# A hybrid diffusion step on one core: the last expert scatter handed over bank by bank, and the final norm computed on turned rows

## The reference, cut to what matters

```python
def rmsnorm(x, g):
    xf = x.astype(jnp.float32)
    y = xf * lax.rsqrt(jnp.mean(xf * xf, axis=-1, keepdims=True) + EPS)
    return (y * g.astype(jnp.float32)).astype(x.dtype)
...
    for i in range(DEPTH):
        ...
        hc2 = rmsnorm(xc, norm2_g[i]) * (1 + ac2) + sc2
        hl2 = rmsnorm(xl, norm2_g[i]) * (1 + al2) + sl2
        xc = xc + gc2 * moe(hc2, router_w, router_b, moe_wg[i], moe_wu[i], moe_wd[i])
        xl = xl + gl2 * moe(hl2, router_w, router_b, moe_wg[i], moe_wu[i], moe_wd[i])
    y_prompt = rmsnorm(xc, final_g)
    y_sample = rmsnorm(xl, final_g)
```

## Time and profile before

| | us |
|---|---|
| median of 3 runs | 1867.9 |
| lowest and highest | 1867.45, 1869.59 |
| profiled execution | 1866.5 |
| its span in the trace | 1864.7 |
| TensorE busy | 1771.1 (95%) |
| VectorE busy | 476.1 (26%) |
| ScalarE busy | 385.3 (21%) |
| moved by DMA | 609.47 MB, 327 GB/s in the mean |

### The profile page before, as it was taken

How to read it: one execution, slowest core, us unless ns; L and a number is a source line. 1 busy time by engine, 2 the same in 40 slices (tenths; PEclk the granted TensorE clock), 3 DMA queues, 4 the chain that set the end, 5 groups by cost and what they waited for, 6 DMA issues and landing times.

```text
span 1864.7 us, 21714 instructions
## 1 busy us (share of the span) xinstructions
PE 1771.1 (95%) x8838; PEld 1034.5 (55%) x8838; DVE 476.1 (26%) x1240; ACT 385.3 (21%) x774; POOL 40.6 (2%) x52
## 2 busy tenths in 40 slices
PE   4999999999999988999999999999999999999996
PEld 2677544446745867854444747864444687544444
DVE  1242511115300242241111244350111252411112
ACT  1232200003102472110001232320000342200002
POOL 1000000000000000000000000000000000000000
PEclk9999999999998988999999999989999999899998
DMA  9979699997998225379999895869999819699992
GB/s 323 365 284 387 261 422 427 427 418 275 354 368 300 99 105 202 140 286 428 427 426 415 313 332 208 328 243 424 427 427 422 311 67 383 250 423 426 427 426 96
DMA packets 134407, 609.47 MB, mean 327 GB/s; under 512 B 12486, under 2 KB 19278, under 8 KB 109473
## 3 DMA queue, kind: packets, MB, share of 16 engines
q1 hardware_dynamic: 117264, 589.32, 79.4%
q10 hardware_dynamic: 12528, 10.70, 1.8%
q0 software_dynamic: 4512, 8.02, 1.1%
HBM read 606.15 MB, written 8.92 MB: 330 GB/s over the span
## 4 chain that ended last, share of the span: by engine, by line
PE 87%; DVE 4%; DMA 3%; ACT 3%; issue 1%; ACTq 1%; DVEq 0%; SPq 0%; POOLq 0%
PE PS L1535 23%; PE PS L961 22%; PE PS L1546 12%; PE PS L1499 7%; PE PS L991 4%; PE PS L1043 3%; PE PS L1011 2%; DVE arena L2085 2%; DMA ring<-in_moe_wg 1%; PE PS L1540 1%; PE PS L1479 1%; DMA ring<-in_w_mod 1%; PE PS L1029 1%; DVE RS L1696 1%; PE PS L1521 1%
## 5 line engine op out<-in xcount | busy, mean ns | idle before, releaser
L1535 PE MATMUL PS<-ring,arena 128*64 128x512 f32 x1280 | 375.5, 601 | 1.6 <-DMA ring<-in_moe_wg 1.5
L893 ACT ACTIVATE arena<-PS 128x512 f32<-128x512 f32 (+1 forms) x130 | 70.6, 543 | 797.7 <-PE PS L1526 349.9
L1535 PEld LDWEIGHTS PS<-ring,arena 128*64 128x64 f32 x1280 | 116.9, 138 | 179.2 <-issue 179.1
L2085 DVE TENSOR_TENSOR arena<-arena,PS 128x512 f32<-128x512 f32 x32 | 33.5, 1046 | 638.9 <-PE PS L1535 638.9
L961 PE MATMUL PS<-HS,ring 128*128 128x256 f32 x768 | 176.6, 388 | 3.0 <-DVE HS L1788 1.7
L1535 PE MATMUL PS<-arena 128*64 128x512 f32 x576 | 169.6, 594 | 0.0
L961 PEld LDWEIGHTS PS<-HS,ring 128*128 128x128 f32 x768 | 147.0, 194 | 30.2 <-issue 8.6
L1499 PE MATMUL PS<-arena 128*128 128x256 f32 (+3 forms) x688 | 144.6, 361 | 5.1 <-ACT arena L893 3.7
L961 PE MATMUL PS<-arena,ring 128*128 128x256 f32 x640 | 140.1, 381 | 2.5 <-ACT arena L659 1.1
L1546 PE MATMUL PS<-ring,arena 128*64 128x512 f32 x640 | 141.7, 595 | 0.0
L1499 PEld LDWEIGHTS PS<-arena 128*128 128x128 f32 (+1 forms) x688 | 112.2, 190 | 44.2 <-issue 22.7
(11 more groups left out here) (341 smaller groups left out, 1711.9 us busy)
## 6 DMA issues: line engine op xcount, KB each, us to landing
ring<-in_w_mod SPq DMA_DIRECT2D x48, 2048.0 KB, 15.7
ring<-in_moe_wu SPq DMA_DIRECT2D x41, 2048.0 KB, 21.0
ring<-in_moe_wd SPq DMA_DIRECT2D x41, 2048.0 KB, 21.6
ring<-in_moe_wg SPq DMA_DIRECT2D x41, 2048.0 KB, 20.3
arena<-in_moe_wg SPq DMA_DIRECT2D x24, 2048.0 KB, 18.1
HS<-in_moe_wu SPq DMA_DIRECT2D x12, 2048.0 KB, 18.3
arena<-in_moe_wu SPq DMA_DIRECT2D x12, 2048.0 KB, 20.3
arena<-in_moe_wd SPq DMA_DIRECT2D x12, 2048.0 KB, 24.9
```

The costliest lines, as they stand in the source:

```text
L893: A(dst, src, func).then_inc(S(sem), 1)
L1535: ins = mm(PS[64 * e:64 * e + 64, b, :], XG[:, k, 64 * e:64 * e + 64], w[:, k], start=(k == 0), stop=(k == KD - 1))
L2085: tt(by_k(HID), row(SG), row(bank(here[1])), ALU.mult).then_inc(S("hid"), 1)
```

## The change

- The eight matmuls of a scatter gave one increment, at the end, in each of the 32 pairs. Now only the last scatter of a layer increments the semaphore, once for each bank, after every second matmul, and the residual waits for the count that covers its column tile. The wait for extra blocks' scatter stays ahead of the residual.
- The final norm no longer uses norm and sumsq. TensorE turns X itself, column tile by column tile as the residual delivers it, into rows in banks 4 to 7 (two banks for each stream). ScalarE squares each bank of 512 with an accumulator, which gives a sum for each token on its own partition. VectorE adds the two sums of a token, ScalarE takes the root of two values a partition, VectorE the reciprocal, and then multiplies each bank in PSUM by that scalar and by final_g, writing to XR. Each stream is stored after its two banks.
- final_g is not loaded as a column at the start, but at the end, to all 128 partitions (512 KB), into slot 0 of the weight ring, by SyncE, once TensorE is through with the last weights, and in SyncE's stream behind the wait for the extra blocks.

```diff
@@ SyncE
-            sp.wait_ge(S("y_sb"), 4)
-            sp.dma_start(O["y_prompt"][0], XR[:, 0]).then_inc(S("out"), 16)
-            sp.dma_start(O["y_sample"][0], XR[:, 1]).then_inc(S("out"), 16)
+            sp.wait_ge(S("down"), 2 * NPAIR * DEPTH)
+            sp.dma_start(FG, I["final_g"].partition_broadcast(P)).then_inc(S("load_b"), 16)
+            for s, y in enumerate(("y_prompt", "y_sample")):
+                sp.wait_ge(S("y_sb"), 2 * s + 2)
+                sp.dma_start(O[y][0], XR[:, s]).then_inc(S("out"), 16)
@@ ScalarE
-            for name, src, n in (("cc", I["c_ctx"], 8), ("cl", I["c"][0], 8), ("fin", I["final_g"], 8),
+            for name, src, n in (("cc", I["c_ctx"], 8), ("cl", I["c"][0], 8), 
...
-            norm(2 * DEPTH)
-            act.wait_ge(S("back"), 32 * DEPTH)
-            for k in range(KD):
-                act.wait_ge(S("xn"), KD * 2 * DEPTH + k + 1)
-                run(A(H[:, k], H[:, k], ACT.Copy, scale=prm("fin", 1, k)), "h0")
-            for j in range(4):
-                c, s = j // 2, j % 2
-                act.wait_ge(S("yT"), j + 1)
-                run(A(XR[:, s, 512 * c:512 * c + 512], bank(2 * s + c), ACT.Copy), "y_sb")
+            run(A(sm(636, 1)[0:1], eps1, ACT.Sqrt), "scalar")
+            for j, (s, c) in enumerate(((0, 0), (1, 0), (0, 1), (1, 1))):
+                act.wait_ge(S("yT"), 2 * c + s + 1)
+                run(A(SQ[:, 0:2].rearrange("p a b -> p (a b)"), bank(4 + 2 * s + c), ACT.Square, accum_out=YSS[:, s, c:c + 1]), f"y_sq{j}")
+            after(act, "y_sum")
+            run(A(YR, YSS[:, :, 0], ACT.Sqrt, bias=c_("eps"), scale=1.0 / D), "y_root")
@@ TensorE
-                    if t == 7:
-                        ins.then_inc(S(sem), 1)
+                        if sem and t % 2:
+                            ins.then_inc(S(sem), 1)
...
-            sumsq(2 * DEPTH)
-            for c in range(2):
-                pe.wait_ge(S("h0"), KD * 2 * DEPTH + 4 * c + 4)
+            for k in range(KD):
+                pe.wait_ge(S("x"), KD * 2 * DEPTH + k + 1)
                 for s in range(2):
-                    for k in range(4 * c, 4 * c + 4):
-                        ins = tp(bank(2 * s + c, P * (k % 4), P * (k % 4) + P), H[:, k, T * s:T * s + T], ident)
-                    ins.then_inc(S("yT"), 1)
+                    ins = tp(bank(4 + 2 * s + k // 4, P * (k % 4), P * (k % 4) + P), X[:, k, T * s:T * s + T], ident)
+                    if k % 4 == 3:
+                        ins.then_inc(S("yT"), 1)
@@ VectorE
-            def residual(sem, base, l, vec, src):
+            def residual(sem, base, l, vec, src, each=1):
 
                 for m in range(KD):
-                    if sem:
-                        v.wait_ge(S(sem), base + m + 1)
+                    v.wait_ge(S(sem), base + m // each + 1)
...
-                v.wait_ge(S("scatter"), n0 + 8)
                 v.wait_ge(S("x_scatter"), before + nx)
-                residual(None, 0, l, 5, lambda m: bank(m // 2, N2 * (m % 2), N2 * (m % 2) + N2))
+                residual("scatter", 4 * l, l, 5, lambda m: bank(m // 2, N2 * (m % 2), N2 * (m % 2) + N2), each=2)
...
-            norm(2 * DEPTH)
+            after(v, "y_sq3")
+            run(tt(YSS[:, :, 0], YSS[:, :, 0], YSS[:, :, 1], ALU.add), "y_sum")
+            after(v, "y_root")
+            run(v.reciprocal(YR, YR), "dve")
+            v.wait_ge(S("load_b"), 64)
+            v.wait_ge(S("back"), 32 * DEPTH)
+            for s in range(2):
+                for c in range(2):
+                    run(stt(XR[:, s, 512 * c:512 * c + 512], bank(4 + 2 * s + c), YR[:, s:s + 1], FG[:, 512 * c:512 * c + 512], ALU.mult, ALU.mult), "y_sb")
```

More of the change, by code:

```diff
@@ L179 @@
     "vector_step": ["zero_rows", "prm", "a_ropek0", "l_abs", "l_rows", "l_ac", "g_sm", "g_am0", "g_am1", "g_am2", "g_at_sb0", "g_at_sb1", "g_rn0", "g_rn1",
-                    "a_ropek3"],
-    "scalar_step": ["cs", "l_rowexp", "l_n_sb", "l_nT_sb", "g_u_sb", "g_se", "g_gate", "g_root0", "g_root1"],
+                    "a_ropek3", "y_sum"],
+    "scalar_step": ["cs", "l_rowexp", "l_n_sb", "l_nT_sb", "g_u_sb", "g_se", "g_gate", "g_root0", "g_root1", "y_sq0", "y_sq1", "y_sq2", "y_sq3", "y_root"],
 }
@@ L300, in program @@
         ROOM = [ring[:, r].rearrange("p a b -> p (a b)") for r in range(RING)] + [arena[:, 9608 + 4096 * e:13704 + 4096 * e] for e in range(2)] + [HS[:, :].rearrange("p a b c -> p (a b c)")]
+        FG = ROOM[0][:, 0:D]
+        YSS, YR = sm(0, 2, 2), sm(8, 2)
         MP = [ar(8000, 512), ar(8000, 512), ar(12288, 512), sq(1536, 512), ar(8000, 512)]
@@ L463, in load @@
                 if n == 1:
-                    sp.wait_ge(S("load_p"), 16 * 12)
+                    sp.wait_ge(S("load_p"), 16 * 11)
                     sp.wait_ge(S("load_x"), 32)
@@ L972, in _ @@
             pe.nop().then_inc(S("x_scatter"), 1)
-            pe.wait_ge(S("load_p"), 16 * 12)
+            pe.wait_ge(S("load_p"), 16 * 11)
             for j in range(3):
@@ L1547, in down, with scatter @@
                     return ins
-                def scatter(par, sem, first=False, ts=range(8)):
+                def scatter(par, sem=None, first=False, ts=range(8)):
                     for t in ts:
@@ L1573, in pair @@
                             pe.wait_ge(S("ys"), 2 * n)
-                            scatter(1 - par, "scatter", first=(i == 1), ts=range(6))
+                            scatter(1 - par, first=(i == 1), ts=range(6))
                     if more and not first:
@@ L1579, in pair @@
                     if not first:
-                        scatter(1 - par, "scatter", first=(i == 1), ts=range(6, 8))
+                        scatter(1 - par, first=(i == 1), ts=range(6, 8))
                     if more:
@@ L1634, in moe @@
                         ins.then_inc(S("x_down"), 1)
-                        pe.wait_ge(S("scatter"), q0 + 8)
+                        pe.wait_ge(S("scatter"), 4 * (l + 1))
                         pe.wait_ge(S("x_a"), x_step(before, i, "x_ys"))
```

## The result

The changed kernel took 1849.24 us in the median of 4 runs (1847.65 to 1853.81), the kernel before beside it 1868.74 (1867.45 to 1870.73): ratio 0.9899, 95% interval 0.9880 to 0.9918. Two later comparisons of the same two kernels gave 0.9931 (0.9903 to 0.9958) and 0.9928 (0.9909 to 0.9947); over all of them the medians are 1854.5 (14 runs) and 1868.0 (83 runs), 13.6 us apart. The ratios are each from one comparison; the pool mixes comparisons that ran on different chips. So two things want explaining: what the change is worth, and where the rest of the first 19.5 came from.

What follows compares the result with a forecast made beforehand. TensorE carries 87% of the chain, so gains lie where it runs dry: passages 5.0, end 6.3 and start 0.2 sum to 11.5 us, taking the median from 1867.9 to 1856.4. Range 1853.0 to 1861.5, 8 in 10.

Steps and rivals of the forecast that it cites:

- Passages: Three passages from a layer's experts to the next layer's norm: bank signals save 5.0 us, bounds 0 and 8.4.
- ScalarE is late next: In the passages, ScalarE's Sqrt table limits the first square, leaving gains of 1.60, 1.53 and 1.79 us.
- the rival of 2.8 us a passage: Passages: were ScalarE free earlier, the scatter limits and up to 2.8 us each is won, 1853; chance 0.05.
- The end: From last residual to last store: new final norm and stores save 6.3 us, bounds 4.2 and 7.3.
- The stores' term: End of program: y_prompt's store gets 1.6 us of lead, so the second's wait shortens by 0.7 us, bounds 0 and 1.3.
- The rival of a final norm that is not shorter: End: squares and scalings out of PSUM cost 1.5 us each, adding 4.5 us, 1860.9; chance 0.05.
- final_g: Late 512 KB broadcast load before the final scalings: costs nothing, with 9.5 us of cover; beyond that, one for one.
- The rival on the other side: End: final_g's broadcast lands late, up to 29.6 us, giving 1876.5; chance 0.04 for eating the gain, 0.06 for later still.
- The start: Program start: without final_g's column load ahead of it, x_sample may land sooner; 0.2 us less, bounds 0 to 0.4.
- Weight waits: Experts' weight stream: waits for loads swallow the passages' gain, leaving 6.5 us, 1861.4; chance 0.12 with idle bank signals.
- the prediction's sign of being wrong: In a later layer: TensorE waiting more than 1.5 us for a weight would show the forecast wrong.
- The sum and its range: Whole kernel: 11.5 us less than the median 1867.9, so 1856.4; range 1853.0 to 1861.5 to hold 8 in 10.

Runs made afterwards that it cites:

- e6: Changed kernel with ScalarE's part of the extra blocks left out in layers 0 to 2; ratio to the kernel before 0.9912 (5 runs).
- e2: Kernel before with only the new final norm and its late load of final_g, scatter handed over whole; 1860.14 us, ratio 0.9965.
- e7: Changed kernel with one part undone: both stores wait for all four scalings; single execution, 1848.98 us.
- e9: Changed kernel, unaltered, measured and traced a third time against the kernel before; ratio 0.9928.
- e10: Kernel before, unaltered, measured against itself and traced a third time; ratio 0.9984.
- e5: Changed kernel with 23 dummy products on TensorE where it stands idle; 1849.85 us against 1865.65 for the kernel before, ratio 0.9913.

## Why the prediction was right or wrong

- **Passages: mis-sized, 5.0 for 6.5.** The mechanism held and the first squares came when it said. The step that failed was "as both go at 0.52 a column": 0.52 was VectorE's pace, which ScalarE had followed in the earlier trace rows. Freed from it, squares are 0.45 apart, 0.5 us less over eight, in each of three passages: 4.9 + 3 x 0.47 + the 0.2 of layer 0's slip make about 6.5. The trace of before had that pace, in its first norm:

```profile
41.74 3.55 ACT L606 ACTIVATE HS<-X 128x256 f32<-128x256 f32 x8
```

  And that "ScalarE is late next" was only half of it: TensorE's sums behind its scatter are late within 0.1 us of the same time, as e6 shows. By that the rival of 2.8 us a passage, with ScalarE free, falls too.
- **The end: right.** 6.3 forecast, 6.55 in the trace, 6.5 in e2. Squares 0.72 (0.72), scalings 0.78 (0.79), the last store's issue 5.9 us after the residual's last column (6.0). The stores' term was 0.9 (0.7), by e7. The rival of a final norm that is not shorter, with dear operations out of PSUM, did not occur.
- **final_g: right.** Hidden; landed in 3.7 us, whole. The rival on the other side had no ground. Of the Trainium skill's two statements ("DMA: Bandwidth & Descriptors") neither was tested for its own sake. In the load's two busiest us, 1831.4 to 1833.4, the 16 DMA engines were busy for 0.77 and 0.75 in the mean, so more than a few took part; that all sixteen did is not shown.
- **The start: 0.2 forecast, nothing found.** x_sample was issued sooner (7.33 for 7.60) and landed 10.3 us later instead of 9.7; TensorE took it up at 17.62, after 17.37 before. So its landing did not follow its issue, here or in the other traces (10.1 to 10.3 without final_g's load ahead, 9.4 to 9.8 with it). The 1.15 us by which the changed kernel led at the first norm came again only in e7 (47.25), and not in its own other traces (48.72 and 48.86, against 48.38, 49.38 and 48.71).
- **Weight waits: a rival that hardly mattered.** For the up weights TensorE waited 3.1 us in all where it had been 1.5, in three places: 1.3 ahead of the first passage, 1.6 in layer 1, 0.2 in layer 2. The 1.6 is 0.1 past the prediction's sign of being wrong, but the kernel before waited 2.7 and 3.3 us in its other traces, and between the passages the stretches grew by 0.4 us or less where a passage gave 2.1. That the 1.5 was the only wait for a weight was not so: the trace of before has 6.3 us more for ring<-in_w_mod, all in the first 60 us.
- **The sum and its range: this is where it failed.** The step that failed is the last one, from the added terms to the median and its range. It took the clock and the spread of executions at nothing beyond 0.2%, as if the rest of the kernel would take what it took in one execution. Passages and end are 13.1 us, which makes 1854.8 of 1867.9; the pooled median is 1854.5, inside the forecast's range. The first comparison's 19.5 has some 6 us more. In its pair of traces they lie in stretches outside the change where the granted clock differs, 1.3, 2.9 and 1.7 us in the mLSTM's halves and the extra block, and e9 and e10 show that such differences belong to the execution, not the kernel. The kernel before alone spread over 1860.5 to 1875.5 us; three runs within 0.12% of each other had hidden that. The trace of before had a granted clock of 0.97 in the mean and 0.89 in the mLSTM's second half, so that a term for it had a place; how much it differs between executions no single trace could tell.
- **The range against its own bounds.** Bounds of 0 to 8.4 for the passages, 4.2 to 7.3 for the end and 0 to 0.4 for the start reach from 1851.8 to 1863.7, not from 1853.5 to 1859.5 as the prediction says. 1849.2 lies below these as well.
- **What stays open.** Why the first four runs of the changed kernel all fell on the short side is not known. At equal clock they still gain some 2 us more than the two parts are worth. e5 and e6, which differ little from the changed kernel, gave 0.9913 and 0.9912, between the first comparison's 0.9899 and the later 0.993. A small part of the gain beyond 13.1 us is not ruled out.

## What to carry to other kernels

When a wait goes, read each follower's own pace from a place where nothing holds it up, and not from the stretch in which it followed the wait: here the squares of the first norm in the trace of before, eight in 3.55 us, would have told 0.45 instead of 0.52. Then ask what else the next engine has in its queue; handing over earlier pays only until the consumer's own earlier work ends. And before believing a difference of under one per cent, cut both traces at common landmarks: a gain in a stretch with the same instructions and another granted clock need not be the change's, and a second and third trace of the unchanged kernels can say so for a few runs' price. Here two traces of each were not enough, and the third told.

## What the runs showed of the hardware that was not expected

- The same 595 TensorE records of the mLSTM's second half took 139.8 to 146.1 us over eleven executions without dummies in them, at granted clocks of 0.94 to 0.89; the 154 of the extra block took 27.2 at 1.00 and 28.9 to 29.4 at 0.94, and nothing between. The level that was granted there differed between executions of one program.
- A broadcast of one 4 KB row of HBM to 128 partitions, 512 KB, landed in 3.6 to 3.9 us after its issue, over eight traces in which no other load was under way.
- A square with an accumulator over 512 elements of PSUM: 0.60 us and 0.20 for the read of the accumulator, overlapping, one each 0.72 us. A scaling by a scalar per partition and by a tensor, 512 out of PSUM: 0.78 us, four in 3.11. The Trainium skill, "VectorE: DVE Perf Modes", has in the section on the TRN2 errata a rule for fp32 operations on two tensors. Carried over to this operation it would give 0.69; the measurement decides.
